# Turning cached attention keys on VectorE through a DRAM buffer, two stages ahead of the attention that reads them

## What is computed

```python
# sub-layer 1: mixer. group A = gated delta rule (8 heads), group B = multi-scale causal pooling
pooled = multiscale_pool(proj[..., COL_U:COL_ZB], ...)   # 4 channel groups, windows 2/4/8/16
o_b = pooled * silu(proj[..., COL_ZB:])
x = x + concat([o_a, o_b]) @ w_out                       # output projection
# sub-layer 2: 4-head cross-attention, head width 512, 256 memory tokens
qx = rmsnorm(x, norm_cross) @ w_cq
scores = einsum('bthd,bmhd->bhtm', qx, mem_k) * 512 ** -0.5
ctx = einsum('bhtm,bmhd->bthd', softmax(scores), mem_v)
x = x + ctx @ w_co
```

## Time and profile before

| | |
|---|---|
| time, median of 3 runs | 1667.03 us (1666.84 to 1667.59) |
| the profiled execution: span from first to last instruction | 1663.2 us |
| TensorE (PE) busy | 1643.0 us, 99% |
| VectorE (DVE) busy | 969.9 us, 58% |
| ScalarE (ACT) busy | 673.3 us, 40% |
| DMA | 229.8 MB, mean 138 GB/s |
| granted TensorE clock | 0.998 |

### The profile page before, as it was taken

The page is one execution under the profiler, slowest core; times in us unless marked ns, Lnnn a source line. Parts: engine busy times, 40 slices in busy tenths (PEclk is TensorE's granted clock), DMA queues, the critical chain, the costliest instruction groups (busy, mean ns, idle before and its releaser), DMA issues.

```text
span 1663.2 us, 31696 instructions
## 1 busy us (share of the span) xinstructions
PE 1643.0 (99%) x12906; PEld 1522.8 (92%) x12906; DVE 969.9 (58%) x1676; ACT 673.3 (40%) x1146; POOL 183.7 (11%) x191
## 2 busy tenths in 40 slices
PE   7999999999999999999999999999999999999998
PEld 5887899999999999999999999999999987499998
DVE  5776446665756647565433343333887753499952
ACT  5566345254442543435322222222343333344542
POOL 0121001111121112111100001111000000001120
PEclk9999999999999999999999999999999999999999
DMA  7898734243232432333333334444223399733462
GB/s 266 261 295 254 219 92 119 55 109 99 70 99 53 115 91 77 91 84 96 101 81 83 86 104 139 132 132 138 62 87 97 98 388 396 229 103 105 126 187 108
DMA packets 277534, 229.79 MB, mean 138 GB/s; under 512 B 10825, under 2 KB 244178, under 8 KB 271970
## 3 DMA queue, kind: packets, MB, share of 16 engines
q1 hardware_dynamic: 277184, 228.42, 44.9%
q10 hardware_dynamic: 258, 0.09, 0.0%
HBM read 201.31 MB, written 27.53 MB: 138 GB/s over the span
## 4 chain that ended last, share of the span: by engine, by line
PE 92%; DVE 4%; issue 1%; ACT 1%; DMA 1%; POOL 0%; SPq 0%; DVEq 0%; ACTq 0%; POOLq 0%
PE pj L287 48%; PE pj L486 10%; PE pj L2203 7%; PE dk L2203 5%; PE pj L2946 2%; PE dk L2515 2%; PE pj L2539 1%; PE dk L2439 1%; PE dk L1819 1%; PE pj L2450 1%; PE pj L2548 1%; PE dk L1272 1%; PE dk L1278 1%; PE dk L825 1%; PE dk L2975 1%
## 5 line engine op out<-in xcount | busy, mean ns | idle before, releaser
L287 PE MATMUL pj<-a_hi,w_high 128*128 128x272 f32 x1792 | 394.1, 301 | 0.0
L287 PE MATMUL pj<-a_hi,w_low 128*128 128x272 f32 x1792 | 370.4, 288 | 0.0
L287 PE MATMUL pj<-a_lo,w_high 128*128 128x272 f32 x1792 | 369.7, 288 | 0.0
L287 PEld LDWEIGHTS pj<-a_hi,w_high 128*128 128x128 f32 x1792 | 280.9, 189 | 13.4 <-issue 8.1
L271 DVE TENSOR_TENSOR w_low<-w_raw,w_high 128x2048 fp32r<-128x2048 f32 x76 | 173.9, 2288 | 192.7 <-ACT w_high L261 192.6
L287 PEld LDWEIGHTS pj<-a_lo,w_high 128*128 128x128 f32 x1792 | 281.6, 189 | 0.0
L287 PEld LDWEIGHTS pj<-a_hi,w_low 128*128 128x128 f32 x1792 | 280.1, 189 | 0.1
L261 ACT ACTIVATE w_high<-w_raw 128x2048 fp32r<-128x2048 f32 x76 | 145.4, 1913 | 57.9 <-PE pj L287 45.9
L2087 ACT ACTIVATE q_high<-q_part 128x512 fp32r<-128x512 f32 x140 | 77.5, 620 | 73.3 <-DVE q_part L2141 37.0
L287 PE MATMUL pj<-mix_hi,w_high 128*128 128x272 f32 x512 | 105.9, 288 | 0.0
L287 PE MATMUL pj<-mix_lo,w_high 128*128 128x272 f32 x512 | 105.5, 288 | 0.0
(11 more groups left out here) (482 smaller groups left out, 3029.5 us busy)
## 6 DMA issues: line engine op xcount, KB each, us to landing
w_raw<-in_w_in_dram SPq DMA_DIRECT2D x48, 1024.0 KB, 5.9
w_raw_wide<-in_w_ck_dram SPq DMA_DIRECT2D x16, 1024.0 KB, 8.6
w_raw_wide<-in_w_cv_dram SPq DMA_DIRECT2D x16, 1024.0 KB, 7.9
w_raw<-in_w_out_dram SPq DMA_DIRECT2D x16, 1024.0 KB, 6.0
q_part<-in_w_cq_dram SPq DMA_DIRECT2D x48, 256.0 KB, 3.6
w_raw<-in_w_co_dram SPq DMA_DIRECT2D x8, 1024.0 KB, 8.3
q_part<-in_w_co_dram SPq DMA_DIRECT2D x32, 256.0 KB, 3.8
xr<-xT_scratch SPq DMA_DIRECT2D x16, 272.0 KB, 6.3
```

Source lines behind the costliest of these rows:

```text
L287: mm = pe.matmul(pj[:, 2 * (q % 2) + b, 0:n], wt[:, k, :], x(k, o, n), start=(k == 0 and m == 0), stop=(k == KT - 1 and m == 2))
```

## The change

- Keys of requests 0 to 4 are turned in ten units during the pool branch (groups 1 to 3), those of requests 5 to 7 in twelve half-size units during the output projection. In a unit SP loads a part of the keys with 32 memory tokens times 8 blocks on each quarter of the partitions, DVE turns 32x32 blocks (`dve.transpose`), and SP stores the result in a DRAM buffer, keysT_d. Four DMAs of 32 partitions each make a load, and four a store; there are two stores to a unit.
- The buffers of the pool units lie where mix_hi's first six rows go, so the parts of mixo are split in another order, now five parts; rows 0 to 5 are split in group 3, tile q = 3, once all units are stored.
- Attention loads keys from keysT_d, turned; the transposes, their copies and kct are gone. There are eight slots. Prompt scores, request scores, contexts and values stand in a new order on PE, with the lists of ACT, DVE and SP to match.
- DVE's loop over j in the output projection is written out.

```diff
+        keysT_d = nc.dram_tensor("keysT_scratch", [NB, P, KT, MEM], F32, kind="Internal").ap()
...
+        kin = take("kin", [BLOCKS, 2 * P])
+        kout = [take(f"kout{i}", [4, BLOCKS, T32]) for i in range(2)]
...
+        def keys_in(sp, dst, b, first, loaded):
+            for i in range(4):
+                cols = slice(first + i * dst.shape[-1], first + (i + 1) * dst.shape[-1])
+                src = t["cache_mem_k"][0, b].rearrange("(g m) h d -> m g (h d)", m=T32)
+                sp.dma_start(dst[i * T32:(i + 1) * T32], src[:, :, cols]).then_inc(loaded.sem, 16)
+        def keys_out(sp, src, b, tile, step, first, n, stored):
+            for i in range(4):
+                dst = keysT_d[b, first * T32:(first + n) * T32, tile + step * i, :].rearrange("(j d) m -> d j m", d=T32)
+                sp.dma_start(dst, src[i * T32:(i + 1) * T32].rearrange("p j g m -> p j (g m)")).then_inc(stored.sem, 16)
+        def sp_keys(sp, u):
+            if 0 < u <= POOL_UNITS:
+                sp.wait_ge(k_turned.sem, k_turned.at(2 * u))
+                keys_out(sp, kout[1], (u - 1) // 2, 8 * ((u - 1) % 2) + 1, 2, 0, 4, k_stored[1])
+            if u < POOL_UNITS:
+                if u == 0:
+                    sp.wait_ge(oa_done, HEADS)
+                keys_in(sp, kin, u // 2, 8 * P * (u % 2), k_in_loaded)
+                sp.wait_ge(k_turned.sem, k_turned.at(2 * u + 1))
+                keys_out(sp, kout[0], u // 2, 8 * (u % 2), 2, 0, 4, k_stored[0])
+        def dve_keys(dve, u):
+            if u >= POOL_UNITS:
+                return
+            dve.wait_ge(k_in_loaded.sem, k_in_loaded.at(64 * u + 64))
+            for f in range(2):
+                at_least(dve, k_stored[f], 64 * u)
+                keys_turn(dve, kout[f], kin[:, :, f * P:(f + 1) * P]).then_inc(k_turned.sem, 1)
...
@@ sp_pool, at the end of slot q; dve_pool alike
+                    if not first:
+                        sp_keys(sp, 4 * (g - 1) + q)
...
-        MIX_PARTS = ((0, 4), (4, 8), (8, 14), (14, 16))
+        MIX_PARTS = ((6, 8), (8, 12), (12, 14), (0, 6), (14, 16))
...
@@ dve_pool
                     if q == 3:
+                        if g == 3:
+                            mix_take_low(dve, 3)
                         dve_windows(dve, g, 0)
+                    if g > 0:
+                        dve_keys(dve, 4 * (g - 1) + q)
...
+        def sp_keys_late(sp, i):
+            u = i - 1
+            if 0 <= u < OUT_UNITS:
+                b, h = divmod(2 * POOL_UNITS + u, XH)
+                sp.wait_ge(k_late_turned.sem, k_late_turned.at(2 * u)) if u else sp.wait_ge(k_turned.sem, k_turned.at(2 * POOL_UNITS))
+                keys_in(sp, kin_late, b, h * XD, k_late_loaded)
+                for f in range(2):
+                    sp.wait_ge(k_late_turned.sem, k_late_turned.at(2 * u + f + 1))
+                    keys_out(sp, kout_late[f], b, 4 * h, 1, 2 * f, 2, k_late_stored[f])
...
@@ dve_out, between split_low and the product's read
+                    dve_keys_late(dve, i)
...
@@ sp_cq, once part 77 of cq is done
+            sp_ktb(sp, 0)
+            load_keys(sp, 0, 0, 8)
+            load_keys(sp, 0, 8, KT)
+            load_keys(sp, 1, 0, 12)
...
@@ pe_attention
+            pe_prompt_scores(pe, 0)
+            pe.wait_ge(rest_out.sem, rest_out.at(7 * PAIRS))
+            scores(0)
+            scores(1)
             pe_prompt_scores(pe, 1)
+            turn(0)
+            context(0, every)
+            scores(2)
+            scores(3)
+            turn(1)
+            context(1, every)
+            scores(4)
+            pe_prompt_scores(pe, 2)
+            for b in (5, 6, 7):
+                scores(b)
+            pe_prompt_scores(pe, 3)
             pe.wait_ge(prs_ready.sem, prs_ready.at(1))
...
             turn(2)
+            for b in (0, 1, 2):
+                values(b)
             context(2, every)
+            turn(3)
+            for b in (3, 4, 5):
+                values(b)
+            context(3, every[0:2])
             values(6)
-            turn(3)
             values(7)
-            context(3, every[0:2])
```

More of the change, by code:

```diff
@@ L1928, in body @@
                                              ALU.mult, ALU.subtract).then_inc(h_low, 1)
-            body(0)
-            with dve.Fori(1, 4) as j:
+            for j in range(4):
                 body(j)
@@ L2325, in build @@
         vtb = [take(f"vtb{i}", [2, XD]) for i in range(2)]
[L2326 to L2333, removed]
@@ new lines, in build, with load_keys, load_values @@
+        VALUES_AT = (("hi_end", 2), ("lo_end", 2), ("raw_b", 2), ("high", 2), ("w", 3), ("q_a", 1), ("q_b", 1), ("raw_b", 3))
+        def load_keys(sp, b, first, end):
+            slot, _ = KEYS_AT[b]
+            sp.dma_start(kept_keys[slot][:, first:end, :], keysT_d[b, :, first:end, :]).then_inc(kv_loaded[slot].sem, 16)
+        def load_values(sp, b):
+            slot, _ = VALUES_AT[b]
+            for m in range(2):
+                sp.dma_start(kept_values[slot][:, m, :], t["cache_mem_v"][0, b, m * P:(m + 1) * P, :, :].rearrange(
+                    "p h d -> p (h d)")).then_inc(kv_loaded[slot].sem, 16)
@@ L2519, in pe_attention, with scores @@
         def pe_attention(pe):
-            pe_sample_keys(pe)
+            def scores(b):
+                loaded(pe, b, KEYS_AT)
+                pe.wait_ge(qm_ready.sem, qm_ready.at(b + 1))
+                for d in range(DT):
+                    for h in range(XH):
+                        mm = pe.matmul(pj[h * NS:(h + 1) * NS, 0, 0:MEM], qmb[b % 2][:, DT * h + d, :],
+                                       kept_keys[KEYS_AT[b][0]][:, DT * h + d, :],
+                                       start=(b == 0 and d == 0), stop=(b == NB - 1 and d == DT - 1))
+                mm.then_inc(sk_done.sem, 1)
             def turn(h):
@@ new lines, in dve_attention @@
+            queries(dve, 0)
+            queries(dve, 1)
+            maxima(0)
+            queries(dve, 2)
+            over_sums(0)
+            queries(dve, 3)
+            maxima(1)
+            take_turned(0)
+            for d in range(DT):
+                if d == 2:
+                    over_sums(1)
+                take_context(0, d)
+            queries(dve, 4)
+            queries(dve, 5)
+            take_turned(1)
+            for d in range(DT):
+                take_context(1, d)
@@ new lines, in dve_attention @@
+            queries(dve, 6)
+            maxima(2)
+            queries(dve, 7)
+            over_sums(2)
+            sample_softmax()
+            maxima(3)
+            dve.wait_ge(prt_ready.sem, prt_ready.at(1))
+            probabilities(dve, 0)
+            take_turned(2)
+            for b in range(1, 4):
+                probabilities(dve, b)
+            for d in range(DT):
+                if d == 2:
+                    over_sums(3)
+                    for b in range(4, 7):
+                        probabilities(dve, b)
+                take_context(2, d)
```

301 lines of the change are left out of this document (135 added, 166 removed).

## The result

The changed kernel takes 1712.95 us (median, 1712.14 to 1715.78) beside 1666.93 for the kernel before on the same chip: a ratio of 1.028, with an interval of 1.0265 to 1.0292. The forecast was 1653, in a range of 1641 to 1673. The span of the profiled execution grew by 48.0 us, from 1663.2; the time lies 1.8 us above it and not 3.8, so it grew by 46.0.

A forecast was written before the change was run, and what follows sets the result against it. The prediction took TensorE to bound the kernel, DMA second in attention. Its terms -24 + 5.3 + 2.6 + 2.6 = -13.5, rounded to -14, gave a span of 1649 and a time of 1653 us, range 1641 to 1673.

The forecast's parts named there:

- Bound: Whole kernel: TensorE is the limit, working 1643 of 1663.2 us; in attention DMA is second, just below it.
- parts 1 and 2: Attention: transposes leave PE (29.2 us) and its work is reordered; stage minus 24 us, bounds minus 26 and minus 17.
- 1.2 + 0.9: Attention, head 0: wait in us before its context, with head 1's maxima (1.2 us reduce) ahead on DVE.
- there is no slack: Attention's DMA at 420 to 425 GB/s just meets PE at the last values; a 2% slower queue costs 1.5 us.
- DMA bounds attention: Rival: at 400 GB/s or less the last values land 6 us late or more; stage gains 18, time 1659; chance 0.11.
- Part 3: Pool branch, ten key units: loop of 13.5 us against PE's 13.1 a tile; 5.3 us more, bounds 0 and 16.
- A 1 KB run lies between, and I take 3.3 us: Pool unit's 1 MiB load: time between 3.7 us for 512-byte runs and 2.5 for 8 KB runs.
- half a store 1.6: Pool unit's loop on SP: each half of a unit's store counts 1.6 us, twice in the 13.5.
- The rival's loop: Rival: 32-partition transfers run at half rate (212 GB/s), so the key loop takes 16.8 us; time 1682; chance 0.20.
- The walk through the ten units: Pool branch: first load issued at 826.7, landing at 830.7; the next 13.3 us apart, or 16.3 across a slot q = 0.
- Part 4: Mixer rows split in group 3, q = 3, ahead of the last windows, delaying PE's ux turn: 2.6 us, bounds 1 and 4.
- Part 5: Output projection, twelve half units: loop 12.9 us against 12.0 a tile, costing 2.6 us; bounds 0 and 10.

The follow-up runs named there:

- Experiment 8: Experiment 1's kernel with the next stage's first two weight tiles issued behind the attention's last values: 1645.71 us, ratio 0.987.
- experiment 2: Changed kernel with each unit's four key loads going to 128 partitions instead of 32, keys in a wrong order: 1685.02 us, ratio 1.011.
- experiment 3: Experiment 2's kernel with the pool branch's key stores reading 128 partitions as well: 1684.06 us, ratio 1.010.
- experiment 4: Changed kernel with narrow loads and turns but no stores of turned keys, attention loading from the cache itself: 1656.81 us, ratio 0.994.
- experiment 7: Changed kernel with as many stores but a quarter of their bytes (half in output projection), attention loading from the cache: 1700.0 us, ratio 1.020.
- experiment 1: Changed kernel without its 22 key-turning units, attention loading as many bytes unturned from the cache: 1652.49 us, ratio 0.991.
- experiment 5: Changed kernel with the next unit's load ahead of the second four stores, in the output projection also ahead of weights: 1679.73 us, ratio 1.008.
- 10: Changed kernel with the next load right behind the first four stores, ahead of weights, rows and parameters, plus Experiment 8's edit: 1659.54 us, ratio 0.996.

## Why the prediction was wrong, by its own steps

**Bound and parts 1 and 2.** Right in kind. The order was as drawn (PE waits 2.1 us ahead of the contexts of heads 0 and 1, where the sum had 1.2 + 0.9). The stage gained 17.6 us and not 24. The step "there is no slack" was right and its figure wrong: DMA gave 399 GB/s on the mean from 1399 to 1499 (seven stretches of 10 to 15 us) and not 420 to 425, least at its end. The kernel before had itself given 418 on the mean from 1343 to 1403, below the range that the sum took. PE waited 4.4 us for the last values, where 1.5 were priced, and the half clock behind that wait cost 4.1, a term that the sum did not have. So the rival "DMA bounds attention" was right in kind, and that its 18 us came is in part luck: it had 6 us of waiting and no clock. Experiment 8 shows the kind: with two MiB moved behind the last values 6.8 us come back.

**Part 3 is the step that failed**, its loop of 13.5 us, which was 16.2. From one unit to the next it ran as 1.3 us for a turn and its semaphore, 9.0 of issuing on SP and 6.5 until the last load landed, 16.8 for the first. Two terms are off, and both on the low side. "A 1 KB run lies between, and I take 3.3 us": 5.2 us alone, some 1.9 more, of which experiment 2 returns 1.4 a unit. I had costed the rate by run length and put the width into a rival, on the evidence of one store; a store's row says nothing of a load (experiment 3 finds no price on width for stores at all). And "half a store 1.6" counted a store as its bytes: SP's 12 issues were put at 0.42 us each, 5.0 us, beside the bytes, while with the weights' one they take 8.9 and lie in the loop, ahead of the last load's landing; without stores the loop is 12.8 (experiment 4), with a quarter of their bytes 14.7 (experiment 7). The rival's loop (16.8 us, 1682) had the right length by half the reason, which is luck: it slowed the stores by their width, which had no price, and left out the issuing, which had. The walk through the ten units also starts too early: with its own terms (1.3 + 3.3 + 0.6) the first load lands at 831.9 and not 830.7, and VectorE began on it at 834.7.

What the loops did to PE: in the pool branch it waited 24.6 us for w_low, where 1.3 were forecast, and 2.8 for pw, where 5.4 were; in the output projection 12.9, where 2.6 were. Both are above their bounds of 16 and 10, and the clock comes on top: 10.9 us behind the waits of the pool branch, 6.3 behind those of the output projection.

**The price of the loop** was too low in the rival too. 3.7 us a unit over ten, less slack, made 34; the pool branch and the output projection together lost 65.6. Of that 22.0 is slower matmuls, 18.9 of it the clock behind half of the stalls, a term that no case had. Set against the rival's 39 with parts 4 and 5, 43.6 of idle time is near. Its 1682, 4.6 for that difference, the 22.0, and 6.4 for the smaller gain in the attention, less the 2.0 by which the time lies nearer to the span, make 1713.

**Part 4** was right as a mechanism; forecast 2.6 us (bounds 1 and 4), idle 3.0 in experiment 1, 4.5 with everything else there. In the changed kernel PE waits 3.9 us there and loses 1.7 to the clock, and the last unit's store stands ahead of it:

```profile
997.94 4.75 DMA keysT_scratch<-kout
...
1002.85 2.94 ACT mix_hi L1784
1005.82 3.56 DVE mix_lo L1789
```

**Part 5**: loop 12.9 forecast, 14.3 measured, by the same two terms (experiment 2 returns 1.0 of it, with wide loads); experiment 5 takes it to PE's 12.0 by the order alone, with loads as narrow and stores as many.

What stays open: why the clock fell behind a wait of 1.9 us and not behind one of 2.3; why a store issues in 0.44 us on a free queue and in 0.9 behind a weight tile, which held with a quarter of the bytes too; and 3 of the 22.0 us.

## What to carry to other kernels

When work is added to a queue that waits inside itself, write down the whole cycle (wait, issue of each DMA, bytes ahead, landing, turn) with issue times as part of it, and compare it with the tile; then put the load first in the cycle, since that alone was worth 33 us here and 47 with the tile's other transfers behind it. A loop that is 3 us too long can cost more than 3 us a turn, because TensorE came back from half of its stalls at half clock. Where a stage is freed from one engine, look at what the next limit moves in it that is not needed there: two weight tiles behind the last values were worth 6 to 7 us (experiments 8 and 10) for two moved lines.

## What the runs showed of the hardware

- A load whose four DMAs write 32 partitions each moved at about 200 GB/s alone (160 to 241), over 128 partitions at 250 to 306, with the same 1 KB runs; stores out of 32 or 128 partitions made no difference in time (1685.0 and 1684.1 us).
- DMA issues on SP took 0.43 to 0.48 us each on a free queue (four in 1.76 and in 1.92), but four stores behind a weight tile's transfer took 3.67, and four loads behind these 3.00. With a quarter of the bytes such stores took 3.77.
- After waits of 2.8 and 4.1 us TensorE's granted clock was 0.50 for some 3 us of work (6 matmuls a us and not 10; 3.41 us and not 1.90 for sixteen). In the changed kernel it fell behind ten of 20 waits from 826 to 1408, the shortest of 1.9 us, and not behind waits of 2.1 and 2.3.
- Eight DMAs issued from ACT cost that engine 3.8 to 5.7 us of its own work.
